# Expert outputs stored to two rows per token and added in the last stage, in place of an adding scatter

## What is computed

```python
x = x + y                               # token mixer; kept in DRAM as x2
h2 = rmsnorm(x, g_ffn)
# pairs (token, expert): 2 per token, sorted by expert, padded to blocks
hid = silu(xb @ w_gate[e]) * (xb @ w_up[e])
yb  = hid @ w_down[e]                   # one block, one expert
y   = zeros(T + 1, D).at[buf_tok].add(yb * buf_w)
out = rmsnorm(x + y, g_final)
```

## Time and profile before

| What | us |
|---|---|
| median of 3 timed executions | 1685.16 (1683.69 to 1685.24) |
| span of the profiled execution, first to last instruction | 1681.4 |
| median less that span (what lies around it) | 3.8 |
| parts one and two, up to the first transpose of gathered rows | 1029.5 |
| blocks, from there to the last scatter's issue | 614.5 |
| from the last scatter's issue to the first load of the last part | 11.5 |
| last part, from its first load to the end | 25.9 |

### The profile page before, as it was taken

One profiled execution on the slowest core, in us unless ns is written; L12 is line 12 of the kernel. 1 busy time (PEld: TensorE's weight loads), 2 busy tenths in 40 slices (PEclk: granted clock), 3 DMA queues, 4 the chain that ended last, 5 costly groups with the idle time before them and its releaser, 6 DMA issues. The chain is left out here.

```text
span 1681.4 us, 25555 instructions
## 1 busy us (share of the span) xinstructions
PE 1519.8 (90%) x8198; PEld 1272.6 (76%) x8198; DVE 1050.2 (62%) x1523; ACT 880.8 (52%) x1187; POOL 352.3 (21%) x492
## 2 busy tenths in 40 slices
PE   6999999999999998999999923999999999999980
PEld 5888899988889998888899912666766666666660
DVE  4665444536644443565444543888988888888863
ACT  4644433355444334644433313777777777777752
POOL 1212111002221110112121022223222222322223
PEclk9999999889999997999999856999999999999995
DMA  6224343322334333224333255999999999999966
GB/s 223 76 89 165 104 139 124 109 96 87 104 141 150 114 101 140 85 83 163 116 113 127 76 178 192 383 374 372 375 382 374 376 378 380 377 373 379 382 214 234
DMA packets 72849, 355.14 MB, mean 211 GB/s; under 512 B 10881, under 2 KB 11154, under 8 KB 48034
## 3 DMA queue, kind: packets, MB, share of 16 engines
q1 hardware_dynamic: 58562, 313.72, 50.6%
q0 software_dynamic: 9824, 25.28, 6.4%
q10 hardware_dynamic: 4368, 14.94, 2.3%
HBM read 326.09 MB, written 28.28 MB: 211 GB/s over the span
## 5 line engine op out<-in xcount | busy, mean ns | idle before, releaser
L1169 DVE TENSOR_TENSOR wlo<-est,whi 128x2048 fp32r<-128x2048 f32 x193 | 440.4, 2290 | 110.9 <-ACT whi L1165 84.1
L1165 ACT ACTIVATE whi<-est 128x2048 fp32r<-128x2048 f32 x193 | 368.4, 1916 | 146.4 <-DMA est<-wexp 104.5
L718 DVE TENSOR_TENSOR w<-stage,w 128x1024 fp32r<-128x1024 f32 x175 | 224.3, 1309 | 79.9 <-ACT w L482 78.1
L482 ACT ACTIVATE w<-stage 128x1024 fp32r<-128x1024 f32 x175 | 178.5, 1054 | 126.4 <-PE ps L959 116.4
L1524 PE MATMUL ps<-whi,xT 128*96 128x512 f32 x512 | 205.6, 401 | 21.7 <-DVE xT L1474 21.7
L1526 PE MATMUL ps<-whi,xT 128*96 128x512 f32 x512 | 203.5, 398 | 0.0
L1525 PE MATMUL ps<-wlo,xT 128*96 128x512 f32 x512 | 202.6, 396 | 0.0
L957 PE MATMUL ps<-w,hT 128*128 128x384 f32 x576 | 199.1, 346 | 0.0
L959 PE MATMUL ps<-w,hT 128*128 128x384 f32 x576 | 193.0, 335 | 0.0
L958 PE MATMUL ps<-w,hT 128*128 128x384 f32 x576 | 192.8, 335 | 0.0
L957 PE MATMUL ps<-hT,w 128*128 128x384 f32 x408 | 141.4, 347 | 8.5 <-issue 5.0
(11 more groups left out here) (214 smaller groups left out, 2754.1 us busy)
## 6 DMA issues: line engine op xcount, KB each, us to landing
est<-wexp SPq DMA_DIRECT2D x193, 1024.0 KB, 13.1
stage<-wmix SPq DMA_DIRECT2D x175, 512.0 KB, 4.2
H<-x_all SPq DMA_DIRECT2D x12, 512.0 KB, 8.2
XR<-x_all SPq DMA_DIRECT2D x9, 512.0 KB, 6.0
x_scratch<-XR ACTq DMA_DIRECT2D x9, 512.0 KB, 5.4
h_scratch<-H ACTq DMA_DIRECT2D x9, 512.0 KB, 6.2
cx<-x_scratch SPq DMA_DIRECT2D x9, 512.0 KB, 7.0
y_all<-co ACTq DMA_DIRECT2D x9, 512.0 KB, 6.2
```

What stands on the lines that cost most here:

```text
L482: act.activation(whl[w % 2][0][:, q * PIECE:(q + 1) * PIECE], stage[r % STAGE][:], ACT.Copy)\
L718: vec.tensor_tensor(whl[w % 2][1][o], stage[r % STAGE][:], whl[w % 2][0][o].bitcast(F32), ALU.subtract).then_inc(w_lo, 1)
L1165: act.activation(whi[q][:], est[q][:], ACT.Copy).then_inc(e_hi[q], 1)
L1169: vec.tensor_tensor(wlo[q][:], est[q][:], whi[q][:].bitcast(F32), ALU.subtract).then_inc(e_lo[q], 1)
```

## The change

- Each token has two rows in a new DRAM tensor `y_dram`: the first expert's result goes to row t, the second's to row 1152 + t. The list holds these rows as targets. The scatter is a plain indirect store, without an add.
- Padding places of the list now name a row beyond the end (1152 for the gather, 2304 for the store), and both indirect transfers get a bound, so that such rows are skipped. `gX` is cleared once, ahead of the first gather, so that skipped rows hold numbers.
- The 48 rows of each half of `y_dram` that belong to no token are set to zero at the start of the program, by two transfers of zeros in place of one into the spare rows.
- The last part loads three tiles of 512 KB per 128 rows (`cx`, and two `cy`) in place of one. VectorE adds the two `cy` to `cx`, then ScalarE sums squares as before. `cy` and `co` are rings of three: SP waits with the `cy` of tile t until tile t-3 has been added (`c_done`), VectorE waits with `co` until the store of tile t-3 has landed (`c_st`). ScalarE issues a tile's store one tile later, not two.

The core of the diff:

```diff
@@ empty_list
-    s[:, 1] = ROWS + np.arange(LIST + 2 * P) % TB
+    s[:, 0] = ROWS
+    s[:, 1] = 2 * ROWS
@@ gather
             pool.indirect_dma_start(out=gX[:], out_offset=None, in_=h2_dram,
-                                    in_offset=bass.IndirectOffsetOnAxis(ap=tix[:, 0:1], axis=0)).then_inc(gx_in, 16)
+                                    in_offset=bass.IndirectOffsetOnAxis(ap=tix[:, 0:1], axis=0),
+                                    bounds_check=ROWS - 1, oob_is_err=False).then_inc(gx_in, 16)
@@ block2, gpsimd
             rows_of(pool, 0, True)
+            pool.memset(gX[:], 0.0).then_inc(gx_set, 1)
+            pool.wait_ge(gx_set, 1)
             gather(pool, 0, True)
@@ scatter
-                pool.indirect_dma_start(out=x2_dram, out_offset=bass.IndirectOffsetOnAxis(ap=pix[:, 1:2], axis=0),
-                                        in_=yS[:], in_offset=None, compute_op=ALU.add).then_inc(y_st, 16)
+                pool.indirect_dma_start(out=y_dram, out_offset=bass.IndirectOffsetOnAxis(ap=pix[:, 1:2], axis=0),
+                                        in_=yS[:], in_offset=None,
+                                        bounds_check=2 * ROWS - 1, oob_is_err=False).then_inc(y_st, 16)
@@ block4, sync
                 sp.dma_start(cx[t][:], x2_dram[t * P:(t + 1) * P]).then_inc(c_x[t], 16)
+                for k in range(2):
+                    if t >= 3:
+                        sp.wait_ge(c_done, t - 2)
+                    sp.dma_start(cy[k][t % 3][:], y_dram[k * ROWS + t * P:k * ROWS + (t + 1) * P]).then_inc(c_x[t], 16)
@@ block4, vector
+                vec.wait_ge(c_x[t], 48)
+                vec.tensor_tensor(cx[t][:], cx[t][:], cy[0][t % 3][:], ALU.add).then_inc(c_add, 1)
+                vec.wait_ge(c_add, t + 1)
+                vec.tensor_tensor(cx[t][:], cx[t][:], cy[1][t % 3][:], ALU.add).then_inc(c_done, 1)
+                if t:
+                    normed(t - 1)
```

More of the change, by code:

```diff
@@ L149, in build @@
           y_all, raw_out, fin_out):
-    x2_dram = nc.dram_tensor("x2_scratch", (ROWS + TB, D), F32).ap()
+    x2_dram = nc.dram_tensor("x2_scratch", (ROWS, D), F32).ap()
+    y_dram = nc.dram_tensor("y_scratch", (2 * ROWS, D), F32).ap()
     h2_dram = nc.dram_tensor("h2_scratch", (ROWS, D), F32).ap()
@@ L297, in build @@
         cx = [at(f"cx{i}", [P, D]) for i in range(TILES)]
-        co = [at(f"co{i}", [P, D]) for i in range(TILES)]
+        co = [at(f"co{i}", [P, D]) for i in range(3)]
         cq = at("cq", [P, 3 * TILES])
         cscr = at("cscr", [P, D])
+        cy = [[at(f"cy{k}{i}", [P, D]) for i in range(3)] for k in range(2)]
         assert place[0] <= oT_end + 4 * 2 * EP * EPC
@@ L424, in _ @@
             sp.dma_start(list_dram, list_init).then_inc(l_init, 16)
-            sp.dma_start(x2_dram[ROWS:ROWS + TB], x_all[TILES][0:TB]).then_inc(x2_pad, 16)
+            for k in range(2):
+                sp.dma_start(y_dram[k * ROWS + DEC_SEQ:k * ROWS + FIRST_META], x_all[TILES][0:FIRST_META - DEC_SEQ])\
+                  .then_inc(x2_pad, 16)
             for r in range(STAGE, AHEAD):
@@ L1143, in build @@
         pool_seen = sem("pool_seen")
+        gx_set = sem("gx_set")
         gx_in = sem("gx_in")
@@ L1195, in _ @@
                 sp.wait_ge(h2_st[j], 16 * (SUPER + 1))
-            sp.wait_ge(x2_pad, 16)
+            sp.wait_ge(x2_pad, 32)
             sp.dma_start(gfin[:], g_final.partition_broadcast(P)).then_inc(r_in, 16)
@@ L1246, in _ @@
             for k in range(2):
-                for c in range(2):
-                    mark(vec.tensor_copy(tokid[:, :, k, c], cst3(C_TOKID, TILES)))
+                mark(vec.tensor_copy(tokid[:, :, k, 0], cst3(C_TOKID, TILES)))
+                mark(vec.tensor_scalar(tokid[:, :, k, 1], cst3(C_TOKID, TILES), float(k * ROWS), None, ALU.add))
             for t in range(TILES):
@@ L1598, in build @@
         c_x = [sem(f"c_x{t}") for t in range(TILES)]
+        c_add = sem("c_add")
+        c_done = sem("c_done")
         c_sum = sem("c_sum")
@@ L1602, in build @@
         c_out = sem("c_out")
-        c_st = sem("c_st")
+        c_st = [sem(f"c_st{i}") for i in range(3)]
         part.close()
@@ L1625, in store @@
                 act.wait_ge(c_out, t + 1)
-                act.dma_start(y_all[t], co[t][:]).then_inc(c_st, 16)
+                act.dma_start(y_all[t], co[t % 3][:]).then_inc(c_st[t % 3], 16)
             for t in range(TILES):
-                act.wait_ge(c_x[t], 16)
+                act.wait_ge(c_done, t + 1)
                 if t:
@@ L1632, in _ @@
                 act.activation(cscr[:], cx[t][:], ACT.Square, accum_out=cq[:, t:t + 1]).then_inc(c_sum, 1)
-                if t >= 2:
-                    store(t - 2)
-            store(TILES - 2)
+                if t >= 1:
+                    store(t - 1)
             store(TILES - 1)
-            act.wait_ge(c_st, 16 * TILES)
+            for i in range(3):
+                act.wait_ge(c_st[i], 16 * (TILES // 3))
         @block4.vector
@@ L1642, in _, with normed @@
             vec.wait_ge(g_scaled, 4)
-            for t in range(TILES):
[L1644 to L1647, removed]
+            def normed(t):
+                vec.wait_ge(c_rstd, t + 1)
+                if t >= 3:
+                    vec.wait_ge(c_st[t % 3], 16 * (t // 3))
+                vec.scalar_tensor_tensor(co[t % 3][:], cx[t][:], cq[:, 2 * TILES + t:2 * TILES + t + 1], gfin[:],
+                                         ALU.mult, ALU.mult).then_inc(c_out, 1)
+            for t in range(TILES):
+                vec.wait_ge(c_x[t], 48)
[4 more added lines that the diff above has]
+                    normed(t - 1)
+            normed(TILES - 1)
         part.close()
```

## The result

The changed kernel takes 1691.34 us (median; 1687.9 to 1694.27) against 1685.16 us before: a ratio of 1.0038, with a 95% interval of 1.0028 to 1.0049. The profiled execution spans 1689.3 us against 1681.4, 7.9 us more. The time lies 1.7 us under the 1693 predicted, but several of the terms behind it were off and nearly cancelled.

The account below looks back on a forecast made before the run. Blocks were taken as a near-equal race of DMA and TensorE, DMA binding later ones and the last part. Blocks -18.6, last scatter -1.7, last part +28.2 gave +7.9 on 1685.2: 1693.1 us, predicted 1693, range 1686 to 1707.

Parts of the forecast that it names:

- the sum: Blocks: 18.68 - 0.85 - 0.4 = 17.4 us per block on DMA, under TensorE's 17.67, so TensorE is late next.
- half of that excess: Blocks: 1 to 10 average 18.11 us; an earlier `pix` removes half the excess over 17.67, giving 17.89 per block.
- Rival A: Every block at TensorE's floor, 17.67 us, early stalls all from late `pix`; blocks give 25.2, whole 1686.5; chance 0.17.
- 160 to 209: Blocks' store: ns per plain 4 KB row, bracketed by an output store's row and a gather's, expected nearer the store.
- the forecast's own method: Blocks' store: cost counted as weight loading displaced by 96 rows; 1.0 to 1.25 us plain against 1.93 adding.
- The 0.4 for skipping: Blocks: us per block gained from skipped padding rows, ends 0 (only the last engines freed) and 0.8.
- The barrier behind it stays: Between last scatter and last part: the barrier was taken to remain, with no change in time counted for it.
- the forecast's 1.7: Last scatter: us gained, 1.25 from faster rows and some 0.4 from skipped rows and earlier `pix`; ends 0.4 and 2.2.
- 54.1 us forecast: Last part: its length with 27 loads at 1.26 us each, in place of 25.9, 28.2 us lost.
- the wait for `c_st`: Last part: VectorE's wait for an output buffer comes three tiles, 15 us, after that store, so the ring does not bind.
- The 3.8 us between span and median: Whole kernel: the median before stood 3.8 us above the profiled span, and this was carried over to the forecast.
- Rival B: No relief of DMA: plain rows displace as gathered ones, padding frees only last engines; blocks gain 0 to 6; chance 0.15.

Follow-up runs that it names:

- experiment 1: Changed kernel with plain stores and the last part's two adds kept, but padding rows gathered and stored again, without the clear of gX: 1692.39 us, ratio 1.0043.
- experiment 2: Kernel before with padding rows skipped in gather and store, the store still adding and the last part the old one: 1684.78 us, ratio 0.9996.
- Experiment 4: Changed kernel without the last part's 18 loads and 18 adds of expert outputs (`cy`): 1667.11 us, ratio 0.9895.

## Why the prediction was right, and where steps of it were not

**The blocks: the mechanism was right, the size too small.** 18.6 us were forecast and 24.8 came. TensorE took over as the bound, as the sum said, but "half of that excess" over the floor in blocks 1 to 10 was to stay. None stayed: 18.11 became 17.69 us there. The step that failed is the reading of that mean. In the kernel before seven of these nine blocks were at the floor already (17.65 to 17.68 us), and ScalarE waited for `pix` in them too, by up to 3.5 us. The excess stood in two blocks, of 18.91 and 20.41 us. TensorE's waits in them are not for the hidden rows behind `y_out`: in the first it waited for VectorE's copies of the gathered rows, in the second for a gather, whose issue took 5.61 us on GpSimd.

```profile
1109.86 0.47 PE L1524 MATMUL ps<-whi,xT 128*96 128x512 f32 x1 [1.03 <-DVE xT L1474]
...
1145.54 5.61 POOL L1183 DMA_INDIRECT gX<-h_scratch,tix  x1 [0.41 <-issue]
...
1159.09 0.88 PE L1535 MATMUL ps<-cst,gX 96*128 96x96 f32 x8 [1.69 <-DMA gX<-h_scratch,tix]
```

Such a gather stands in kernels of either form (last section), so up to 2.7 of the 24.8 us belong to that one execution and not to the change. Whether late `pix` slowed VectorE in the other block is not shown. Rival A named the floor in every block, and it came about, in experiment 1 too; that it came by way of `pix` is not shown either. Its counter-argument, that VectorE would be busy over 90% of a block, was true (330.25 of 364 us) and did not matter.

**What the store's form is worth was near the upper end.** The row takes 160 ns, the lower end of 160 to 209. By the forecast's own method the store costs the weights 1.0 instead of 1.93 us, a gain of 0.93 a block where 0.85 was taken. The 0.4 for skipping was wrong: for the adding store it is 0 within the noise (experiment 2), the end that the prediction had kept for padding that frees only the last engines. With 0 the same sum gives 18.68 - 0.93 = 17.75, still next to the floor, so the wrong half cost the forecast little. It also fits the last blocks, where weights come late again.

**The barrier: the other step that failed.** "The barrier behind it stays" took its price as fixed. The last store's landing gave 1.6 us, near the forecast's 1.7, but not by its parts: 1.25 of that were the form's and 0.4 for skipped rows and an earlier `pix`, while without skipping the store lands as soon (3.70 us in experiment 1, 3.64 in the changed kernel). The drain in the barrier grew by 4.8. No row shown of before gave the drain's length, and no bound was put on it; the trace had it, 5.62 us, in the source view of the barrier's line.

**The last part: right.** 54.1 us forecast, 53.5 measured. The last `cy` tile was to be there 43.9 us after the first load's issue; its first add starts at 44.4 (1635.80 to 1680.22). An add takes 1.23 us, not 1.31. Loads and output stores between them took the DMA engines' whole time from 1636 to 1679 us:

```profile
q1 hardware_dynamic: 3870, 14.12, 83.2%
q10 hardware_dynamic: 804, 2.97, 16.9%
```

Experiment 4 confirms the price less directly: without the reads the last part is 23.8 us shorter, and not 27.6, because the three output buffers cost 3.8 us once the loads no longer cover them. The prediction had put "the wait for `c_st`" at nothing for the changed kernel, and there its view of waits shows none.

**The start: 1.3 us, forecast 0.** The clear of `gX` took 0.97 us and stayed under the wait for `tix`. 1.0 of the 1.3 us is there at the barrier ahead of the second part, before the clear (GpSimd's drain at 954.0 against 953.0), and other kernels with the same clear start like the one before (1072.26 in experiment 4, 1073.07 in experiment 2). Nothing shows that the change does it.

**Why the total was near.** 6.2 us more gained in the blocks stand against 4.8 in the drain and 1.3 at the start, with some tenths elsewhere. Rival A's 1686.5 had the blocks right and missed by the two others. A forecast with the right blocks and the same blind spot would have been 1687. The 3.8 us between span and median were too much as well: in every execution with both on record the time is 1.7 to 1.9 us over its span, so the profiled execution of the kernel before was some 2 us faster than its median. On the spans the forecast's +7.9 is met to a tenth, which is luck; the 1.7 us by which the median falls short is this term. Rival B's range begins at 1706 by its own terms, not 1707; nothing hangs on that.

## What to carry to other kernels

Where two engines race, a relief of the one that is late is worth at most the distance to the other: here 25 us, and an edit that pays for it with 28 us of loads that nothing covers loses. The same edit won 12 us once those loads were taken apart into what depends on the last store and what does not, and once the barrier ahead of them was replaced by one semaphore; 7 of the 12 the barrier gives without the edit. Give the kernel before the same side gains, or they are put down to the edit. Look at single blocks before a mean is shared out among causes. Read each barrier's own rows, the drains too, before its price is taken as fixed.

## What was not expected of the hardware

GpSimd's drain ahead of the last part has a length of its own, which repeats to the nanosecond: 5622 ns in three kernels with adding indirect stores, 10441 or 10436 in seven with plain ones (one of them with three adding stores at the end), 7827 without stores. When it stands at the program's end it takes 0.61 us more (6232 and 11051 ns). It delays the program only where something waits behind it. What it counts stays open.

One gather's issue is long. In eight of the thirteen profiled executions, of kernels with adding and with plain stores, one of the 32 gathers takes 4.9 to 5.9 us to issue on GpSimd; no other takes over 3.6. Six of the eight fall into blocks 1 to 31, and the block it falls into takes 19.2 to 21.9 us. Why it comes is not shown.

A skipped row still leaves a packet: of the 96 rows of the changed kernel's last store 66 went out as 4 KB packets and 30 as packets of 4 bytes (46 such packets in all, of which 16 go with a full store too), and q0 has 9824 packets in all, before as after.
